# Decoder trunk on one core: squares of x summed through PSUM, the partition sum half a tile earlier, the root ahead of two weight highs, the stores of x spread between eight weight loads

## What is computed

```python
def rmsnorm(x, g):
    y = xf * lax.rsqrt(jnp.mean(xf * xf, axis=-1, keepdims=True) + EPS)
    return (y * g).astype(x.dtype)
def swiglu(x, w_gate, w_up, w_down):
    return (silu(x @ w_gate) * (x @ w_up)) @ w_down
# each layer:
x = x + 0.5 * rmsnorm(swiglu(rmsnorm(x, g[0]), ffn1...), g[1])
mix, new_state = token_mixer(rmsnorm(x, g[2]), state, ...)
x = x + rmsnorm(mix, g[3])
x = x + 0.5 * rmsnorm(swiglu(rmsnorm(x, g[4]), ffn2...), g[5])
```

## Time and profile before

| | us |
|---|---|
| median of 3 runs | 2165.89 |
| lowest, highest | 2163.85, 2167.8 |
| the profiled execution's own time | 2166.59 |
| its span, first to last instruction | 2164.9 |
| PE busy | 2106.8 (97%) |
| DVE busy | 1362.9 (63%) |
| ACT busy | 1000.1 (46%) |
| POOL busy | 800.8 (37%) |

### The profile page before, as it was taken

How to read it: one execution, slowest core, us unless ns; L and a number is a source line. 1 busy time by engine, 2 the same in 40 slices (tenths; PEclk the granted TensorE clock), 3 DMA queues, 4 the chain that set the end, 5 groups by cost and what they waited for, 6 DMA issues and landing times.

```text
span 2164.9 us, 45498 instructions
## 1 busy us (share of the span) xinstructions
PE 2106.8 (97%) x18864; PEld 2051.7 (95%) x18864; DVE 1362.9 (63%) x2147; ACT 1000.1 (46%) x2027; POOL 800.8 (37%) x645
## 2 busy tenths in 40 slices
PE   8899999999999999999998999999999999899999
PEld 8899999999899989999988999999998899899998
DVE  5999701666457899951289994026654678999313
ACT  5466522534344546652254664235243545566422
POOL 3421274534324431135433113444332354311442
PEclk9999999999999999999999999999999999999999
DMA  6233443322233423343232334333223233233432
GB/s 186 59 99 98 125 114 92 86 71 66 64 90 102 130 76 101 98 127 97 82 125 77 103 103 129 104 90 81 70 60 98 57 116 116 84 98 101 130 92 78
DMA packets 395245, 209.79 MB, mean 97 GB/s; under 512 B 31920, under 2 KB 385472, under 8 KB 395040
## 3 DMA queue, kind: packets, MB, share of 16 engines
q1 hardware_dynamic: 394896, 206.84, 33.8%
q10 hardware_dynamic: 144, 0.06, 0.0%
HBM read 189.18 MB, written 17.67 MB: 96 GB/s over the span
## 4 chain that ended last, share of the span: by engine, by line
PE 80%; DVE 12%; ACT 2%; DMA 2%; issue 2%; POOL 1%; SPq 0%; DVEq 0%; ACTq 0%
PE ps L1026 45%; PE ps L1038 28%; PE ps L1307 1%; DMA w_raw<-in_ffn_w_gate 1%; DVE xn_lo L2241 1%; POOL w_lo L893 1%; DVE stage L2415 1%; DVE x_ops L2436 1%; DMA w_raw<-in_ffn_w_up 1%; DVE x_ops L2433 1%; DVE x_r L2438 1%; DVE spare L2482 1%; DVE numer L2864 1%; DVE x_ops_f L2418 1%; ACT w_hi L1649 1%
## 5 line engine op out<-in xcount | busy, mean ns | idle before, releaser
L893 POOL TENSOR_TENSOR w_lo<-w_raw,w_hi 128x512 fp32r<-128x512 f32 (+1 forms) x440 | 585.1, 1339 | 775.1 <-ACT w_hi L1649 773.3
L1026 PE MATMUL ps<-xn_hi,w_hi 128*128 128x272 f32 x2496 | 575.2, 297 | 34.6 <-POOL w_lo L893 15.3
L1026 PE MATMUL ps<-xn_hi,w_lo 128*128 128x272 f32 x2496 | 557.7, 290 | 0.0
L1026 PE MATMUL ps<-xn_lo,w_hi 128*128 128x272 f32 x2496 | 557.2, 290 | 0.0
L1649 ACT ACTIVATE w_hi<-w_raw 128x512 fp32r<-128x512 f32 (+1 forms) x440 | 264.4, 605 | 617.9 <-PE ps L1026 462.6
L1026 PEld LDWEIGHTS ps<-xn_hi,w_hi 128*128 128x128 f32 x2496 | 410.3, 191 | 58.9 <-issue 32.5
L1026 PEld LDWEIGHTS ps<-xn_lo,w_hi 128*128 128x128 f32 x2496 | 411.7, 191 | 0.3
L1026 PEld LDWEIGHTS ps<-xn_hi,w_lo 128*128 128x128 f32 x2496 | 410.2, 191 | 0.0
L1038 PE MATMUL ps<-x_ops,w_hi 128*128 128x272 f32 x1920 | 368.9, 288 | 0.3
L1038 PEld LDWEIGHTS ps<-x_ops,w_hi 128*128 128x128 f32 x1920 | 302.0, 189 | 1.7 <-ACT rstd L1882 1.2
L2223 DVE TENSOR_TENSOR acc<-acc,gs 128x544 f32<-128x544 f32 (+1 forms) x45 | 35.2, 782 | 319.6 <-ACT gs L1717 319.0
(11 more groups left out here) (399 smaller groups left out, 3529.4 us busy)
## 6 DMA issues: line engine op xcount, KB each, us to landing
w_raw<-in_ffn_w_down SPq DMA_DIRECT2D x160, 256.0 KB, 2.9
w_raw<-in_w_in SPq DMA_DIRECT2D x120, 256.0 KB, 2.9
w_raw<-in_ffn_w_gate SPq DMA_DIRECT2D x76, 256.0 KB, 2.9
spare_f<-in_ffn_w_gate SPq DMA_DIRECT2D x64, 256.0 KB, 2.9
spare_f<-in_ffn_w_up SPq DMA_DIRECT2D x64, 256.0 KB, 2.9
w_lo_f<-in_ffn_w_up SPq DMA_DIRECT2D x56, 256.0 KB, 2.8
w_raw<-in_ffn_w_up SPq DMA_DIRECT2D x48, 256.0 KB, 2.9
x_aside<-x SPq DMA_DIRECT2D x16, 544.0 KB, 4.8
```

Of the source, the lines that this page charges most:

```text
L893: pool.tensor_tensor(w_lo[:, q % RING, 0:m], w_raw[:, q % RAW, 0:m], w_hi[:, n % RING, 0:m].bitcast(F32), ALU.subtract).then_inc(w_split, 1)
L1026: mm = pe.matmul(pair(p)[:, a, :], w, z[:, half(a)], start=(k == 0 and j == 0), stop=(k == chunks - 1 and j == 2))
```

## The change

Four edits. (1) The running sum of the squares is kept in PSUM, `pair(3)`, instead of `acc`; only the last add writes `acc`. (2) `pe_pre_sum` stands after chunk 7 of unit 3 (`OPEN`), four chunks earlier. (3) In ACT's order `act_pre` stands ahead of the highs of blocks 12 and 13. (4) SP issues load 9, put 0, load 10, load 11, put 1, load 12, load 13, put 2, load 14, load 15, put 3, load 16, and then a load of the pair and a plain load in turn (17, 18, 19). Code that was never run (`BY_POOL`) is removed.

```diff
             else:
                 sp.wait_ge(x_kept, 10)
-            put(0)
-            sync_load(sp, n_up + 9)
-            put(1)
-            sync_load(sp, n_up + 10)
-            put(2)
-            sync_load(sp, n_up + 11)
-            put(3)
-            sync_load(sp, n_up + 12)
+            for c in range(4):
+                sync_load(sp, n_up + 9 + 2 * c)
+                put(c)
+                sync_load(sp, n_up + 10 + 2 * c)
             for j in (0, 2, 3):
                 sync_load_pair(sp, l, which, 0, j)
-            for i in range(13, 16):
-                sync_load(sp, n_up + i)
+                sync_load(sp, n_up + 17 + j // 2 + j % 2)
             sp.wait_ge(rstd_ready, v + 1)
             sync_load_pair(sp, l, which, 0, 1)
-            for i in range(16, UP_PLAIN):
+            for i in range(20, UP_PLAIN):
                 sync_load(sp, n_up + i)
...
-                pe_unit(pe, i % 3, n_up + 2 * i, (lambda c: c == 3 and pe_pre_sum(pe, v)) if i == OPEN + 1 else None)
+                pe_unit(pe, i % 3, n_up + 2 * i, (lambda c: c == 7 and pe_pre_sum(pe, v)) if i == OPEN else None)
...
-                if t == OPEN + 1 and c == 3:
+                if t == OPEN and c == 7:
                     pe_pre_sum(pe, v)
...
-            for b in range(9, 14):
+            for b in range(9, 12):
                 act_high(act, n + b)
             act_pre(act, v)
+            for b in range(12, 14):
+                act_high(act, n + b)
...
-                dve.tensor_tensor(acc[:], x_sq[:, 0, :] if c == 1 else acc[:], x_sq[:, c, :], ALU.add).then_inc(x_summed, 1)
+                dve.tensor_tensor(halves(acc[:]) if c == DC - 1 else pair(3), halves(x_sq[:, 0, :]) if c == 1 else pair(3),
+                                  halves(x_sq[:, c, :]), ALU.add).then_inc(x_summed, 1)
```

More of the change, by code:

```diff
@@ L321, in h_tile @@
             return xn_hi[:, t - EARLY_H, :], xn_lo[:, t - EARLY_H, :]
[L323 to L328, removed]
         def x_operand(k, c):
@@ L409, in program @@
         w_low = sem("w_low")
-        w_low_pool = sem("w_low_pool")
         z_kept = sem("z_kept")
@@ L919, in up @@
                 low(4)
[L921 to L930, removed]
                 for t in range(PLAIN_TILES - 1, FC - 1):
                     low(t)
-                    if t < FC - 2:
-                        for k in BY_POOL:
-                            w_lower(t - PLAIN_TILES + 2, k)
                 splits(n_up + UP_ITEMS, n_up + UP_ITEMS + RING)
@@ L1159, in product @@
                 def product(k, bank, before_chunk=None):
-                    pe.wait_ge(w_low_pool if k in BY_POOL else w_low, lows_to(done, k))
+                    pe.wait_ge(w_low, PRODUCTS * done + k + 1)
                     pe_product(pe, n + k, w_slot(w, k, after), k, bank, k in (A11, A22MINUS21, A12), before_chunk)
@@ L2478, in w_lower @@
                 slot = w_slot(w, k, after)
-                if k in BY_POOL:
-                    return
                 dve.wait_ge(w_hi_ready, n + 1)
```

## The result

The changed kernel takes **2146.45 us** (median of 4 runs, 2143.90 to 2147.46); the kernel before, on the same chip, 2165.03 us. The ratio is 0.9911, with a 95% interval of 0.9893 to 0.9928. The profiled execution took 2147.46 us, its span is 2145.7 us, and the mean granted clock is 0.996 (0.992 before). Forecast were 2146.5 us and 19.7 us of gain; the medians differ by 18.6 us and the spans of the two traces by 19.2. A second build of the same text gave 2147.43 us, ratio 0.9913 [0.9896, 0.9930]; its span is 2146.2 us.

What follows compares the result with a forecast made beforehand. DVE's chain from the root to the first pair product was taken to bound the FFNs. A root 27.7 us sooner in all, less 8.0 us of collisions, gave 19.7 us of gain: 2146.5 us, range 2137 to 2156.

Steps and rivals of the forecast that it cites:

- What bounds the kernel: FFNs: DVE's chain from root to first pair product, about 51 us, sets the pace; the root waits for an unrelated weight load.
- The sum 3.0 us sooner: PE in the FFNs: partition sum moved four chunks, 24 matmuls, earlier, so 3.0 us sooner with PE's work unchanged.
- The adds: DVE's six last adds, now in PSUM: 0.75 us each instead of 1.58, ending 3 us ahead of PE.
- The root sooner by 6.2, 6.8, 7.4, 7.3 us: ACT's root ahead of highs 12 and 13, in FFNs v = 0, 2, 3, 5: together 27.7 us sooner.
- The collisions, 2.0 us per FFN: Two POOL splits meet DVE's SBUF steps behind the root: 2.0 us per FFN, bounds 0 and 2.7, 8.0 in all.
- SP's order "at nothing": SP's queue: only the stores move, they land in time for x_mix, the fourth pair load is in time; no cost.
- rival B: Load 13 still late: high 13 blocks silu(0), DVE stands at up(0); gain 3.9 us per FFN, 2150.5 us; chance 0.15.
- The stop at unit 9: PE's wait for a block's low part at unit 9 of an FFN: still there, 3 to 4 us.
- A: No collisions: the two splits miss DVE's steps or freed adds make up for them; gain 27.7 us, 2138.5; chance 0.15.
- C: Root not the limit: a split or slow-clock stop holds the pair product; 2 us or less per FFN, about 2160; chance 0.10.
- D: Slower: adds late at the sum's new place, PE stands at all six sub-layers; 2175.5 us at 2.1 us per add; chance 0.04.
- E: Change doesn't do what it says: high 11 is late, the root hardly moves; within 0.2%; chance 0.03.

Runs made afterwards that it cites:

- e4: Changed kernel with the partition sum back at its old place (unit 4, chunk 3): 2159.04 us.
- e8: From e7: partition sum two chunks sooner, root ahead of high 11, block 11's low on DVE, stores 0 and 1 behind loads 10 and 11: 2139.61 us.
- e7: Changed kernel with the low parts of blocks 12 and 13 made by DVE behind x_mix(0) instead of by POOL: 2146.00 us.
- e9: From e8: DVE instead of POOL also makes the low parts of h tiles 0 and 1 and of block 14: 2131.75 us.
- e10: From e9: DVE also makes the low parts of blocks 15, 16, 17 and of h tile 2: 2125.52 us.
- e6: Kernel before the change with only SP's new order of stores and loads: 2152.25 us, ratio 0.9942.
- e2: Changed kernel with the highs of blocks 12 and 13 put ahead of the root again: 2153.20 us.
- e1: Changed kernel with the running sum's adds kept in SBUF (acc) as before the change: 2155.94 us.
- e3: Changed kernel with SP's old order of stores and loads: 2149.71 us.
- e5: Kernel before the change with only ACT's order changed, the root ahead of highs 12 and 13: 2157.98 us, ratio 0.9969.

## Why the prediction was right, step by step

**What bounds the kernel: right.** In before and after DVE has no gap of over 0.15 us between the second gate and the pair product, in any FFN. Moving the root by 3.0 us moved the pair product by 2.6 to 3.2 us (e4 against the second build), and by 1.5 to 2.2 us it moved 1.3 to 2.0 (e8 against e7), while the distance behind the root stayed within half a us. Shortening DVE's steps behind the root shortened it again (e9, e10). Before, the root waited for a load that it has nothing to do with: e6 and e2 show it from both sides.

**The sum 3.0 us sooner: right.** In v = 2 it stands 8.51 us after the first add, 11.53 before: 3.0.

**The adds: right.** 0.72 to 0.8 us against an estimate of 0.75, with no idle time of PE before the sum. With SBUF adds the stop of v = 2 is 1.65 us where 1.7 was forecast (e1).

**The root sooner by 6.2, 6.8, 7.4, 7.3 us: right, where high 11 is in time.** Measured against the first add of each FFN: 6.2 (v = 0), 6.8 (v = 2), 6.7 (v = 3), 6.8 (v = 5) in the first build, together 26.4 instead of 27.7, and 6.2, 6.8, 7.4 and 7.2 in the second, together 27.5. The step assumed that high 11 is in time for the sum. In v = 2 of the first build it is, by hundredths of a us. In its v = 3 load 10, issued behind put 0, came late (ACT stood 3.25 us for it, 1.96 in the second build), and Ln stood behind high 11.

**The collisions, 2.0 us per FFN: right in kind and nearly in size.** The distance grew by 2.1 us in v = 0, 2.4 in v = 2, 2.5 in v = 3, and by 2.0 to 2.5 in the second build. In v = 5 it grew by 3.4, of which PE's slow clock is about one (below). So 4 x 2.4 = 9.6 us would have been the better term, by the second build 8.9. The page "SBUF — State Buffer" of the Trainium skill (section "SBUF: two separate sides") made it the 2.7 us bound; the rows lie between.

**SP's order "at nothing": right for the landing of the stores, and it hid what the edit is worth.** For the stores the step named only who waits for their landing (`x_mix`, never late). What they do to the loads behind them came in once, as "it comes sooner" for load 11, without a price. Put back into the changed kernel the old order costs 3.3 us, which is within the noise (e3). Done alone the new one is worth 12.7 (e6). "Only the stores move" was wrong too: the three pair loads move behind load 13 as well (rival B has it right), and no run separates them from the stores. The sum of the prediction did contain that gain, since it took the root from the sum and not from the load; but it booked it under ACT's order, which alone is worth 7.0 (e5). Alone, the parts give 12.7 + 7.0 = 19.7 us, so that the change as a whole (18.6) looks like their sum; it is not. Both remove the same wait, for block 13. e4 shows it: with the stores, ACT's order and the adds moved, and only the sum at its old place, the four FFNs last 70.5, 67.2, 67.2 and 67.2 us from first add to pair product, and with ACT's order alone (e5) 70.6, 67.1, 67.2 and 67.2. On top of SP's new order, ACT's order (with the adds in PSUM, which the root does not feel at this place) even costs, 6.8 us from e6 to e4, because the root gains 0.4 to 1.2 us per FFN and the collisions take about 2. Only with both is the sum's place what sets the root, and the 3 us there, worth nothing before (e2, with stores, sum and PSUM moved, is no faster than e6), become worth 12.6 (e4).

**The stop at unit 9:** 3.3 us, in the range said. **The mixers:** they gave nothing, as said (v = 1 lasts 321.16 us before and 321.17 after; v = 4 is above).

**The rivals.** A (no collisions): refuted by the gates and `stage` of v = 2. B: its wait is absent from the changed kernel and shows in v = 2 of e3, at 0.32 us, and of e9, at 0.65. C: refuted by e4 and e8. D: no wait in the changed kernel; with the adds in SBUF 6.4 us of stops (e1). E: refuted by the root, 6.2 to 7.4 us sooner.

**How good is 2146.5 against 2146.45?** Better than its steps. The forecast of the time began at 2165.89 us, and the kernel before measured 2165.03 in the end, so the gain was 18.6 us against 19.7, and the interval of the ratio is itself 8 us wide. In the first build the steps were off by -1.3 us (root) and -1.5 (collisions), with 1 us of clock in v = 5, and the 2.2 us at the start and in v = 4 that came by chance stand against them. In the second build the same two terms are 27.5 - 8.9 = 18.6 us, and the FFNs are 18.6 us shorter: there the sum closes without luck, 1.1 us below the forecast. The mechanism and the size are shown; that the time agrees to 0.05 us is luck.

## What to carry to other kernels

A constant distance from one instruction to another, over stages where the engine between them stops at different places, points to a chain on another engine. Which one, the rows tell: here DVE's, with no gap in them. Then read backwards what its first step waits for, and look whether an in-order engine or queue has put something foreign ahead of it. Price edits in pairs: two that remove the same wait look worth their full sum alone, and a third can be worthless until both are in. Where two engines slow each other at the same memory, giving the bound engine the other's work (0.7 us) can be cheaper than having it done beside it (1.1 us).

## What was not expected of the hardware

**A meeting costs about what is left of POOL's instruction, not a share of DVE's step.** A DVE step with both operands in SBUF, run wholly beside POOL instructions, took 0.43 → 1.62 us (128x272), 0.72 → 1.88 and 0.72 → 1.81 us (128x544): the rows of e9 and e8, 1.1 to 1.2 us more for a step of either size. A whole split inside the two gates cost 1.39 us and inside the two `stage` steps 1.03 (after). Two that caught only the end of a split cost less: with 0.60 us of it left 0.45 us more (e2), with 0.49 us left 0.35 more (e7). POOL's instructions here take 1.3 us undisturbed and up to 1.8 beside DVE, and nothing smaller or larger was run. So a short DVE step pays as much as a longer one, and a chain of short SBUF steps was the worst neighbour of POOL among those measured.

**The other side gains too.** POOL's three splits beside the adds took 4.23 us when these kept their sum in PSUM; with adds in SBUF the same splits took 5.21 us in the trace of before (v = 2, from 727.33).

**The same stop, not the same clock.** A stop of 3.3 us at unit 9 comes in all four FFNs of the changed kernel. The windows of ten us behind each of the four (for v = 0, 2, 3, 5):

```profile
76.00:86.00 10.00, 8.49 (x56) 8.52 (x56) 9.82 (x9) 4.23 (x8) 8.39 (x5) 0.83 0.28 80
766.00:776.00 10.00, 8.97 (x59) 9.00 (x60) 9.79 (x10) 3.76 (x7) 7.94 (x5) 0.83 0.28 80
1136.00:1146.00 10.00, 9.38 (x63) 9.41 (x64) 9.78 (x10) 3.70 (x8) 7.48 (x5) 0.83 0.28 81
1826.00:1836.00 10.00, 9.04 (x50) 9.07 (x51) 9.79 (x10) 3.71 (x8) 7.82 (x5) 0.66 0.27 79
```

Three times 0.17 x 10 = 1.7 us of PE's work are lost, once 0.34 x 10 = 3.4 us. In before there was a third outcome; the windows behind its stops of 3.58 us (v = 3) and 3.33 us (v = 5) at unit 9:

```profile
1149.00:1159.00 10.00, 8.98 (x72) 9.01 (x73) 9.79 (x10) 3.75 (x7) 7.92 (x5) 1.00 0.28 80
1845.00:1855.00 10.00, 8.94 (x71) 8.97 (x72) 9.79 (x9) 3.79 (x7) 7.96 (x5) 1.00 0.27 79
```

Nothing is lost there. In both of these FFNs the clock had fallen before, behind the stop ahead of unit 6 (0.57 over 1124 to 1132 and over 1820 to 1828, 3.4 us each), but that is not what decides: in v = 2 of e1, with no such stop, the granted clock behind 3.32 us at unit 9 was 1.00 too. So a stop of this length cost 0, 1.7 or 3.4 us of work besides itself. PE's idle time before the pair product answers to it: 1.8, 0.25 and 0 us in before and after, in this order. With 1.7 the FFN pays nothing, since DVE's chain ends later than PE anyway; with 3.4, in v = 5, PE reached the pair product last, with no idle time before it, and the distance was 54.4 us instead of 53.4. That is also what took e7's gain in v = 0. What decides between the outcomes stays open: no run here was made for it. In e9 the stops at unit 9 are 1.1 to 1.8 us and the granted clock behind them is 1.00. That is not where its gain comes from: in e8 PE stood 0.25 to 1.8 us for DVE before each of the four pair products, so its clock held nothing up.

**A mixer of two lengths.** In every kernel here whose adds are not late, the mixers v = 1 and v = 4 last 321.2 to 321.5 us, or 322.7 to 322.9 when the granted clock falls for 4 to 5 us in them, as in before (0.57 over 1612 to 1616). The second build of the changed kernel has the long form in v = 1 and the short one in v = 4, the first build two short ones. A difference of 1.5 or 3 us between two traces can be no more than this.
